# Places of the operands of float32r products within a partition of SBUF

## The reference, cut to what matters

```python
def swiglu(h, w13, w2):                       # four times, width 2816
    gate, up = jnp.split(h @ w13, 2, axis=-1)
    return (jax.nn.silu(gate) * up) @ w2
...
z = h @ w_in[l]                               # second block, two layers: ten projections
...
merged = (gates[:, :, 0] * (y_rg @ w_br_rg[l]) + gates[:, :, 1] * (y_ml @ w_br_ml[l])
          + gates[:, :, 2] * (y_xa @ w_br_xa[l]))
x = x + merged @ w_out[l]
...
f = swiglu_2(h2, ffn_w1[j], ffn_w3[j], ffn_w2[j])      # layer 0, width 3584
f = moe_swiglu(h2, router_w, router_b, moe_w1, moe_w3, moe_w2)   # layer 1: 8 experts, 2 per token
```

## Time and profile before

| | us |
|---|---|
| median of 3 runs | 3206.28 |
| lowest and highest | 3204.17, 3206.91 |
| the profiled execution | 3203.32 |
| its span, first to last instruction | 3201.5 |

### The profile page before, as it was taken

How to read it: one execution, slowest core, us unless ns; L and a number is a source line. 1 busy time by engine, 2 the same in 40 slices (tenths; PEclk the granted TensorE clock), 3 DMA queues, 4 the chain that set the end, 5 groups by cost and what they waited for, 6 DMA issues and landing times.

```text
span 3201.5 us, 53354 instructions
## 1 busy us (share of the span) xinstructions
PE 3132.6 (98%) x20750; PEld 2865.1 (89%) x20750; DVE 1983.5 (62%) x2086; ACT 1726.0 (54%) x2031; POOL 1339.4 (42%) x587
## 2 busy tenths in 40 slices
PE   8999999999899999999999999999999999999998
PEld 8998999998699989899999999997888888888887
DVE  6544644544433374274533761738899899898997
ACT  5443445333234344644434456537777777777775
POOL 6753676871057564486887753770000000000000
PEclk9999999999999999999999999999999999999999
DMA  6543554553245443345555433457998998989985
GB/s 238 188 164 126 180 187 164 185 184 132 79 158 185 160 155 136 123 172 188 184 184 184 172 132 132 153 203 284 344 365 341 355 348 340 373 342 337 370 340 214
DMA packets 97231, 704.30 MB, mean 220 GB/s; under 512 B 10929, under 2 KB 10929, under 8 KB 11601
## 3 DMA queue, kind: packets, MB, share of 16 engines
q1 hardware_dynamic: 96768, 700.26, 59.0%
q10 hardware_dynamic: 288, 2.10, 0.2%
q0 software_dynamic: 48, 0.13, 0.0%
HBM read 701.40 MB, written 1.05 MB: 219 GB/s over the span
## 4 chain that ended last, share of the span: by engine, by line
PE 94%; DVE 2%; POOL 1%; ACT 1%; issue 1%; DMA 0%; DVEq 0%; ACTq 0%
PE bank L650 26%; PE bank L651 26%; PE bank L652 26%; PE bank L771 3%; PE bank L1117 2%; PE bank L768 1%; POOL half_lo L612 1%; PE bank L1259 1%; PE bank L736 1%; PE bank L1305 1%; PE bank L785 1%; PE bank L721 1%; PE bank L1277 1%; PE bank L887 1%; PE bank L921 1%
## 5 line engine op out<-in xcount | busy, mean ns | idle before, releaser
L612 POOL TENSOR_TENSOR half_lo<-ring,half_hi 128x1024 fp32r<-128x1024 f32 x582 | 1338.5, 2305 | 812.1 <-ACT half_hi L1390 811.1
L1390 ACT ACTIVATE half_hi<-ring 128x1024 fp32r<-128x1024 f32 x582 | 615.2, 1061 | 793.5 <-PE bank L652 730.3
L650 PE MATMUL bank<-h_hi,half_hi 128*128 128x256 f32 x2928 | 829.9, 283 | 6.5 <-POOL half_lo L612 6.5
L652 PE MATMUL bank<-h_hi,half_lo 128*128 128x256 f32 x2928 | 823.0, 281 | 0.0
L651 PE MATMUL bank<-h_lo,half_hi 128*128 128x256 f32 x2928 | 822.9, 281 | 0.0
L650 PEld LDWEIGHTS bank<-h_hi,half_hi 128*128 128x128 f32 x2928 | 552.8, 189 | 12.4 <-issue 6.4
L651 PEld LDWEIGHTS bank<-h_lo,half_hi 128*128 128x128 f32 x2928 | 551.7, 188 | 0.7
L652 PEld LDWEIGHTS bank<-h_hi,half_lo 128*128 128x128 f32 x2928 | 551.6, 188 | 0.0
L1843 ACT ACTIVATE expert_parts<-ring 128x1024 fp32r<-128x1024 f32 x336 | 337.2, 1055 | 112.3 <-PE bank L652 112.3
L650 PE MATMUL bank<-expert_parts,h_hi 128*128 128x512 f32 x896 | 358.4, 400 | 3.5 <-DVE expert_parts L2594 2.0
L652 PE MATMUL bank<-expert_parts,h_hi 128*128 128x512 f32 x896 | 352.5, 393 | 0.0
(11 more groups left out here) (400 smaller groups left out, 5592.0 us busy)
## 6 DMA issues: line engine op xcount, KB each, us to landing
ring<-stream SPq DMA_DIRECT2D x327, 1024.0 KB, 4.8
ring<-experts SPq DMA_DIRECT2D x168, 1024.0 KB, 6.5
kept<-experts SPq DMA_DIRECT2D x112, 1024.0 KB, 6.9
lent<-experts SPq DMA_DIRECT2D x56, 1024.0 KB, 6.9
lent<-mem ACTq DMA_DIRECT2D x2, 1024.0 KB, 6.8
con<-consts SPq DMA_DIRECT2D x1, 1505.0 KB, 12.1
kept<-x_in SPq DMA_DIRECT2D x1, 1024.0 KB, 5.0
kept<-mem SPq DMA_DIRECT2D x1, 1024.0 KB, 16.1
```

The source lines that it names most:

```text
L612: nc.gpsimd.tensor_tensor(half_lo[:, h % HALVES, :, :], by_tile(ring[:, u % RING, s * HALF:(s + 1) * HALF]), half_hi[:, h % HALVES, :, :]. ...
L650: mm(dst, w_hi, x_hi, start=start, stop=False, skip_group_check=shared)
L652: return mm(dst, w_lo, x_hi, start=False, stop=stop, skip_group_check=shared)
L1390: nc.scalar.activation(half_hi[:, h % HALVES, :, :], by_tile(ring[:, u % RING, s * HALF:(s + 1) * HALF]), ACT.Copy).then_inc(hi_ready, 1)
```

## The change

The padding of the tiles is taken away: `WROW` and `SROW` become 128 columns, so all tiles of a buffer begin at the same place within 512 bytes. Every buffer of a split tensor gets a written place. With `ring` at a multiple of 512 bytes as before, the places within 512 bytes are, after the change: the three buffers of `half_hi` at 0, 64 and 128, and those of `half_lo` likewise; `h_hi` at 0 and `h_lo` at 64; `hid_hi` at 0 and `hid_lo` at 128; the slots' tiles all at 0; `expert_parts` (and `lent`, which lies in the same space) at 64, by a gap of 112 columns; the part of the experts' weights in `half_lo`'s space at 64. Tensors behind `expert_parts` move with it. Operations, shapes, waits, transfers and their order stay. The uses of `half_hi` and `half_lo` change only in how a buffer is named.

```diff
-WROW, XROW, SROW = PARTS + 2, TOK + 0, SLOTS + 2
+WROW, XROW, SROW = PARTS + 0, TOK + 0, SLOTS + 0
...
-        half_rows = [sb(name, [PARTS, HALVES * 8 * WROW], F32R) for name in ("half_hi", "half_lo")]
-        half_hi, half_lo = (a[:, :].rearrange("p (h k c) -> p h k c", h=HALVES, k=8)[:, :, :, 0:PARTS] for a in half_rows)
-        h_rows = [sb(name, [PARTS, max(KT * XROW, 16 * SROW)], F32R) for name in ("h_hi", "h_lo")]
-        h_hi, h_lo = (a[:, 0:KT * XROW].rearrange("p (k t) -> p k t", k=KT)[:, :, 0:TOK] for a in h_rows)
-        hid_hi = sb("hid_hi", [PARTS, 2, 512], F32R)
-        hid_lo = sb("hid_lo", [PARTS, 2, 512], F32R)
-
+        HALF_AT = ((0, 1040, 2080), (96, 1136, 2176))
+        H_AT, HID_AT = (96, 16), (112, 32)
+
+        def row_tiles(a, at, n, row, width):
+
+            return a[:, at:at + n * row].rearrange("p (k c) -> p k c", k=n)[:, :, 0:width]
+
+        half_rows = [sb("half_hi", [PARTS, 3104], F32R), sb("half_lo", [PARTS, 3200], F32R)]
+        half_hi, half_lo = ([row_tiles(a, at, 8, WROW, PARTS) for at in places] for a, places in zip(half_rows, HALF_AT))
+        h_rows = [sb("h_hi", [PARTS, 2144], F32R), sb("h_lo", [PARTS, 2064], F32R)]
+        h_hi, h_lo = (row_tiles(a, at, KT, XROW, TOK) for a, at in zip(h_rows, H_AT))
+        hid_rows = [sb("hid_hi", [PARTS, 1136], F32R), sb("hid_lo", [PARTS, 1056], F32R)]
+        hid_hi, hid_lo = (row_tiles(a, at, 2, 512, 512) for a, at in zip(hid_rows, HID_AT))
+
+        sb("page_gap", [PARTS, 112])
...
-        slot_rows = [a[:, 0:16 * SROW].rearrange("p (k s) -> p k s", k=16)[:, :, 0:SLOTS] for a in h_rows]
-        xs_hi, xs_lo = (slot_rows[0][:, KT * i:KT * (i + 1), :] for i in range(2))
-        hT_hi, hT_lo = ([slot_rows[1][:, KT * i + 4 * j:KT * i + 4 * (j + 1), :] for j in range(2)] for i in range(2))
+        xs_hi, xs_lo = (row_tiles(h_rows[0], at, KT, SROW, SLOTS) for at in (96, 1120))
+        hT_hi, hT_lo = ([row_tiles(h_rows[1], at + 4 * SROW * j, 4, SROW, SLOTS) for j in range(2)] for at in (0, 1024))
...
-                half_rows[1][:, 0:2 * HALF]]
+                half_rows[1][:, 112:112 + 2 * HALF]]
...
-                    nc.gpsimd.tensor_tensor(half_lo[:, h % HALVES, :, :], by_tile(ring[:, u % RING, s * HALF:(s + 1) * HALF]),
-                                            half_hi[:, h % HALVES, :, :].bitcast(F32), ALU.subtract).then_inc(lo_ready, 1)
+                    nc.gpsimd.tensor_tensor(half_lo[h % HALVES], by_tile(ring[:, u % RING, s * HALF:(s + 1) * HALF]),
+                                            half_hi[h % HALVES].bitcast(F32), ALU.subtract).then_inc(lo_ready, 1)
```

More of the change, by code:

```diff
@@ L645, in half @@
                 pe.wait_ge(lo_ready, 2 * BODY * r + (h + 1))
-                return half_hi[:, h % HALVES, :, :], half_lo[:, h % HALVES, :, :]
+                return half_hi[h % HALVES], half_lo[h % HALVES]
             def products(dst, w_hi, w_lo, x_hi, x_lo, start, stop, shared=False):
@@ L704, in opening @@
                                 pe.wait_ge(xg_hi, k // 2 + 1)
-                            mm(b[:, m * 256:m * 256 + 256], half_hi[:, h % HALVES, k, :], h_hi[:, k, :],
+                            mm(b[:, m * 256:m * 256 + 256], half_hi[h % HALVES][:, k, :], h_hi[:, k, :],
                                start=k == 0 and m == 0, stop=False, skip_group_check=True)
@@ L1389, in hi @@
                 act.wait_ge(unit_full[u % RING], 16 * (BODY // RING) * r + 16 * (u // RING + 1))
-                nc.scalar.activation(half_hi[:, h % HALVES, :, :], by_tile(ring[:, u % RING, s * HALF:(s + 1) * HALF]),
+                nc.scalar.activation(half_hi[h % HALVES], by_tile(ring[:, u % RING, s * HALF:(s + 1) * HALF]),
                                      ACT.Copy).then_inc(hi_ready, 1)
```

## The result

The changed kernel takes 3217.01 us (median of 5 runs, 3213.11 to 3219.32) where the kernel before takes 3204.17 (5 runs, 3200.18 to 3206.91): ratio 1.0038, 95% interval 1.0025 to 1.0051. It is slower by 13 us where 38 us of gain were forecast. The time lies in the predicted range, on the other side of no change. The profiled execution took 3217.01 us, its span 3215.2.

What follows compares the result with a forecast made beforehand. The prediction took TensorE's matmul pace, busy in 98% of the span, as the bound. Gains of 31 us (dense) and 8 (experts), 39 in all, took the profiled 3203.3 us to 3164, given as a median of 3168; range 3125 to 3240.

Steps and rivals of the forecast that it cites:

- step 1: Dense float32r products on TensorE: fixed places bring 118.2 ns a matmul to 116.0, a gain of 31 us.
- step 3: ACT's copy, POOL's L612 and DVE's parts write contiguous tiles: 0 to a few ns each, covered by TensorE's time.
- step 4: Plain float32 work, whose pages move by 64 bytes: 0, since its steps don't vary.
- Step 2: Experts' 512-column products on TensorE: 232 ns a matmul becomes 230, a gain of 8 us.
- (b): Places don't matter for TensorE's average, the stream itself loses the time: 3206 us, within 6; chance 0.13.
- (c): Dense products fall on a poor fixed pattern: 119.5 ns, 18 us, with 4 in the experts, 3228 us; chance 0.34.
- (a): The forecast itself: fixed places fall on a pattern near TensorE's short steps, 3168 us; chance 0.52.
- POOL's L612 as releaser of L650: Falsifying sign: TensorE's dense matmuls waiting for POOL's subtraction for more than the 6.5 us of the kernel before.

Runs made afterwards that it cites:

- all_64_above: Changed kernel with every dense weight tile 64 bytes above its stream, and the slots' tiles at 64 above expert weights at 0: 3236.76 us, 1.0108.
- above_64_128_192: Changed kernel with all streams, high and low, at 64 and the three buffers of both halves at 128, 192 and 256: 3209.97 us, 1.002.
- experts_only: Kernel before with only the experts' part of the change (slots' tiles contiguous at 0, expert_parts and the low weights at 64): 3195.86 us, 0.9971.
- padded_halves: Changed kernel with 8 bytes between the tiles of both halves again, first places and all else as changed: 3196.29 us, 0.998.
- high_padded: Changed kernel with 8 bytes between half_hi's tiles again, half_lo left contiguous: 3196.5 us, 0.9976.
- all_at_256: Changed kernel with all streams at 64 and all three buffers of both halves at 256: 3212.95 us, 1.0028.
- low_padded: Changed kernel with 8 bytes between half_lo's tiles again, half_hi left contiguous: 3219.93 us, 1.0053.

## Why the prediction was wrong

Two steps of the sum failed. The forecast was -39 us of span, measured were +14: step 1 gave nothing for its 31 us, the waits that step 3 put at nothing cost 18 us in the dense products, and step 4, also put at nothing, lost 5 us. The experts gave 9 for 8. Step 1 is the larger part of the miss, step 3 is what turned the sign. (The sum itself ends at 3167, not 3168; nothing hangs on that.)

**The step that turned the sign is number 3 of the sum**: contiguous tiles for POOL were "bounded by 0 and a few ns each, covered". Undisturbed, the subtraction took 2.40 us for 2.21 (the medians of the 582), 190 ns more; the mean grew by 216 ns. The cover was worked out as 2.84 - 2.305 us, 0.53 us a half unit, and on average 0.3 us of it are left. But the average is not what pays. POOL's idle gap between two halves is also where DVE gets its turn. Here is one passage of the hidden layer's split, of DVE and POOL, in the kernel before (start, us, engine, line; in brackets the idle time before):

```profile
197.62 2.31 DVE L1995 CAST hid_hi<-hid 128x512 fp32r<-128x512 f32 x1
199.97 0.69 DVE L1997 TENSOR_TENSOR hid_lo<-hid,hid_hi 128x512 fp32r<-128x512 f32 x1
...
197.31 2.33 POOL L612 TENSOR_TENSOR half_lo<-ring,half_hi 128x1024 fp32r<-128x1024 f32 x1 [0.61 <-ACT half_hi L1390]
200.16 2.57 POOL L612 TENSOR_TENSOR half_lo<-ring,half_hi 128x1024 fp32r<-128x1024 f32 x1 [0.51 <-ACT half_hi L1390]
```

The same passage after, and the start of PE's next product:

```profile
200.39 2.51 DVE L2002 CAST hid_hi<-hid 128x512 fp32r<-128x512 f32 x1
202.94 2.92 DVE L2004 TENSOR_TENSOR hid_lo<-hid,hid_hi 128x512 fp32r<-128x512 f32 x1
...
200.08 2.54 POOL L619 TENSOR_TENSOR half_lo<-ring,half_hi 128x1024 fp32r<-128x1024 f32 x1 [0.43 <-ACT half_hi L1397]
202.93 2.38 POOL L619 TENSOR_TENSOR half_lo<-ring,half_hi 128x1024 fp32r<-128x1024 f32 x1 [0.30 <-ACT half_hi L1397]
...
205.91 0.39 PE L657 MATMUL bank<-hid_hi,half_hi 128*128 128x256 f32 x1 [1.33 <-DVE hid_lo L2004]
```

The cast takes 0.43 us alone, and 2.3 to 2.6 us when POOL started first: it ends in POOL's gap. Before, that gap was 0.52 us (199.64 to 200.16), and hid_lo got in ahead of POOL, in 0.69 us. After, it is 0.31 us (202.62 to 202.93), hid_lo starts 0.01 us behind POOL and ends 0.55 us after POOL does, 2.92 us for 0.69. TensorE waits 1.33 us for it, and its next step is 1.5 us longer; that stands at five such places. So 0.19 us on POOL cost 2.2 us on DVE.

The Trainium skill has this lock: its page "SBUF — State Buffer", section "Who interferes with whom", says that DVE and GpSimd share a port pair which whoever starts first holds for the whole instruction, that a cast can take it, and that a DVE instruction with two inputs in SBUF contends with a GpSimd one that reads SBUF. The rows above agree: 0.43 us alone and 2.31 or 2.51 us behind POOL for the cast, 0.69 us and 2.92 us for hid_lo with its two inputs.

The rest of the waits goes the longer way. A run of short operations on `lent` (256 columns) stands on DVE's queue there. In the kernel before, several of them pass in one gap of POOL's (0.29 and 0.43 us each), the next one waits, and DVE reaches sg at 94.61:

```profile
86.41 0.29 DVE L2126 TENSOR_SCALAR lent<-lent 128x256 f32<-128x256 f32 x1
86.73 0.43 DVE L2127 SCALAR_TENSOR_TENSOR lent<-lent 128x256 f32<-128x256 f32 x1
87.19 2.33 DVE L2128 SCALAR_TENSOR_TENSOR lent<-lent 128x256 f32<-128x256 f32 x1
...
94.61 0.68 DVE L1986 TENSOR_TENSOR sg<-bank,rs 128x512 f32<-128x512 f32 x1
```

After, one passes for each subtraction, and sg starts at 99.70. ACT takes its sg at 100.42, with the copies to half_hi queued behind it; POOL waits for these, and PE for POOL:

```profile
88.81 2.38 DVE L2132 TENSOR_SCALAR lent<-lent 128x256 f32<-128x256 f32 x1
91.22 2.38 DVE L2133 TENSOR_SCALAR lent<-lent 128x256 f32<-128x256 f32 x1
93.63 2.51 DVE L2134 SCALAR_TENSOR_TENSOR lent<-lent 128x256 f32<-128x256 f32 x1
96.18 2.50 DVE L2135 SCALAR_TENSOR_TENSOR lent<-lent 128x256 f32<-128x256 f32 x1
...
99.70 0.68 DVE L1993 TENSOR_TENSOR sg<-bank,rs 128x512 f32<-128x512 f32 x1
...
100.42 0.63 ACT L1477 ACTIVATE sg<-sg 128x512 f32<-128x512 f32 x1 [4.69 <-DVE sg L1993]
100.96 1.99 ACT L1397 ACTIVATE half_hi<-ring 128x1024 fp32r<-128x1024 f32 x2
...
102.08 2.46 POOL L619 TENSOR_TENSOR half_lo<-ring,half_hi 128x1024 fp32r<-128x1024 f32 x1 [3.69 <-ACT half_hi L1397]
...
104.59 0.39 PE L657 MATMUL bank<-h_hi,half_hi 128*128 128x256 f32 x1 [1.43 <-POOL half_lo L619]
```

So where the page says that PE waits for POOL, POOL had waited 3.69 us for ACT, ACT for DVE, and DVE for POOL's subtractions, once for each short operation.

**Step 1, the dense products**, was mis-sized: 116.0 ns forecast, 118.1 measured on the average of all, 0.4 us of gain for 31. The loop that the prediction read got slower: one pass of 144 steps runs from the first to the second row,

```profile
48.42 0.29 PE L657 MATMUL bank<-h_hi,half_hi 128*128 128x256 f32 x1
...
65.51 0.29 PE L657 MATMUL bank<-h_hi,half_hi 128*128 128x256 f32 x1
```

17.09 us, 118.7 ns, where it was 118.2; others got faster. The reasoning from single fast steps was the weak point. A fast step beside a slow one need not be a good place; their mean over a few tiles is what a pattern costs. Fixed places gave means between 115.7 and 119.8 ns, and some of these are mixtures of two speeds. With all streams at 64, the other half units at 128 and 256 took 117.8, at 384 117.9, at 192 118.4, at 448 118.6 and at 320 119.8 ns, so the place counts. The distance alone does not tell the pace (64 bytes above the stream gave 119.2 ns in all_64_above and 115.7 in above_64_128_192), and neither does the place alone (113.3 and 117.8 ns for one place). The page "TensorE: Matmul & The Clock Gate" of the Trainium skill, in the section named in the prediction, speaks for places that don't matter; 229.1 against 233.3 ns for the same 512-column products shows that they do, though no run shows by what mechanism.

**Step 2, the experts**, held: 229.1 ns for 231.7, 8.6 us for 8, and an expert of 124.75 us for the 124.7 forecast. DVE did not bind. **Step 4** held for the steps themselves (215.8 ns mean in both), but the plain work lost 5 us to late DVE operands: the second row of the waits after, DVE's `hid`, 9.4 us for 3.7.

**The rivals.** (b) was right for the dense average, by its number and not by its reason. (c) had the sign and not the mechanism: its place was the pace of the dense products and its price 18 us; the pace stayed and the waits took 23 (18 and 5). (a)'s gain exists in the experts alone. The mechanism that decided was written down as what would falsify the forecast, POOL's L612 as releaser of L650 above 6.5 us (now 11.3), but it was given no price and no chance: "a pace of 113 and POOL is still ahead" compared means, and took POOL's duration as a constant of the tile's size.

What stays open: why two contiguous inputs cost POOL 8% (the low half's place and the tiles' order are ruled out; fixed places of the two inputs against each other were run only in steps of 64 bytes, all of them slow, so a fixed offset of 8 bytes is untested), what sets TensorE on 113.3 or 117.8 ns, and why that lower value was met at 128, 256 and 384 and never at 192, 320 and 448. The best version that was run is experts_only; the intervals of padded_halves and high_padded overlap with its own.

## What to carry to other kernels

An engine with slack on the average can still be what a chain depends on: look at the gaps between its instructions, ask who uses them, and price a lengthening of that engine by the size of the gap, not by its busy share. A layout change is a change for every engine that touches the tile, so each of them needs a price from both sides; and parts of a change with different readers (experts and dense products here) are best tried apart, since one gave 9 us that the other lost. And a mean may be a mixture: look at how the single units spread, and at which buffer each of them used, before a theory is built on it.

## What the runs showed of the hardware

- The same float32r products, from the same addresses, run at 113.3 ns or at 117.8 ns a step (256 columns, clock 1.00). With all halves at one place (all_at_256) the two hold for long stretches and all 24 changes stand at a break in the row of products; with three places in turn (above_64_128_192) they alternate without one.
- POOL's subtraction of 128x1024 elements takes 2.40 us with both inputs contiguous and 2.20 us when the high half has 8 bytes between its tiles of 128 columns, whether the output is padded or not (low_padded, high_padded).
- A DVE operation of 256 columns takes 0.29 or 0.43 us, and 2.3 to 2.5 us when POOL's subtraction has started first; the cast of 512 columns 0.43 and up to 2.6.
- Float32r steps of 512 columns were 229.1 ns (stream at 64, weights at 0), 231.7 (before) or 233.3 (stream at 0, weights at 64).
